# Second layer's feed-forward: both halves of the input in one 512-column matmul, with VectorE adding the parts and squaring

## The chip, the core and the metric

The kernel runs on one core of a Trainium2 chip. The metric is the device time of one execution in microseconds (us). A run's time is the median of several executions. One further execution is recorded by the hardware profiler; all rows below come from that one.

## The reference, cut to what matters

The reference is a transformer block followed by a two-layer block. Only the last part of the last layer is touched by the change:

```
def sq_relu_mlp(h, w1, w2):
    return jnp.square(jax.nn.relu(h @ w1)) @ w2
...
        h2 = adaln_norm(x, norm2_g[l], mx[3], mx[4])
        x = x + mx[5] * sq_relu_mlp(h2, w_ff1[l], w_ff2[l])
```

Here `h2` is 256 tokens by 1024 features, `w_ff1` is 1024 by 4096, and `w_ff2` is 4096 by 1024, all float32. In layer 0 the same weights also act on 256 context tokens, so its products have 512 columns; in layer 1 (the last) there are 256.

## The kernel before, in words

**Three products for one.** Every dense product is made from halves. A float32 value is split into a high half (a rounded copy in the type fp32r) and a low half (value minus high). A weight `w` and an input `x` give `wh*xh + wh*xl + wl*xh`: three matmuls of one 128x128 weight tile into one PSUM bank (lines 581, 584 and 586 in `three`). Activations are stored with features on the 128 partitions and tokens along the free dimension, so a layer-1 product has 256 columns. `HH` and `HL` hold the high and low half of the normalised input, `HIDH1` and `HIDL1` (tile HID in the trace) those of the hidden vector.

**The weight stream.** All weights come from memory as one stream of blocks of 128x1024, that is eight 128x128 tiles, 512 KB each. SyncE issues one DMA per block into four buffers `wr`. ScalarE copies a block to `wh` (three buffers, line 433), then VectorE or GpSimd subtracts to give `wl` (three buffers, line 449). `by_pool` says which of the two; in layer 1 it is GpSimd for every block behind the first group of three tiles. Every engine runs its own list in the order in which it was written. `AHEAD = 2`: on ScalarE the high half of the block that is two blocks ahead is made at a fixed place of the list. Since there are three buffers, block n waits until TensorE has finished block n - 3.

**FF1 of layer 1.** The hidden vector has 32 tiles of 128 features, f = 0 to 31. Tiles 0 to 2 are computed together in `dense_group` (lines 486, 490 and 493). From f = 3 on, `dense` computes one tile at a time: eight products over the eight input tiles. Each such f uses exactly one weight block. So there are 29 tiles, 232 products, 29 blocks. For each f the engines do this:

- ScalarE (`act_ff`): makes the high half of block f + 2; waits for the products of f; Relu from PSUM to a scratch tile `tm` (line 2780); waits for the square; copies `tm` to the high half of the hidden tile (line 2783).
- VectorE (`dve_ff`): waits for the Relu; multiplies `tm` by the PSUM bank, which gives the squared positive part (line 2798); waits for the copy; subtracts to give the low half of the hidden tile (line 2801).
- GpSimd: makes the low half of the blocks, one after the other (line 449).

On ScalarE the order is therefore: copy of f - 1, high half of block f + 2, Relu of f, copy of f. Block numbers below are the f that uses the block. The scratch ring `tm` has three tiles, the PSUM ring `main` four banks.

**FF2 of layer 1.** Eight output tiles d of 32 products each. For d = 0 to 6 `wide` is true: `three` gets an output of 512 columns, and since that is wider than `xh` it issues one matmul of `wh` with `xh` and `xl` side by side (line 578, through `beside`, which makes one access pattern of two stretches), then one of 256 columns for `wl` (line 580). The first half of the bank then holds `wh*xh + wl*xh`, the second half `wh*xl`, and VectorE adds both to the result (lines 2721 and 2727). The last tile d = 7 uses three matmuls.

Of the kernel before, what the change touches and what calls it, by code (L numbers as in the profile page):

```python
# [8 lines left out]
ALU = mybir.AluOpType  # L9
ACT = mybir.ActivationFunctionType  # L10
F32 = mybir.dt.float32
F32R = mybir.dt.float32r
# [266 lines left out]
class Program:  # L279
    def __init__(self, nc, ctx, csizes, old):  # L280
        self.nc, self.old = nc, old

        def sb(name, shape, dt=F32):
            return ctx.enter_context(nc.sbuf_tensor(name, shape, dt))
# [27 lines left out]
        self.WL = [sb(f"wl{i}", [128, 1024], F32R) for i in range(NSPL)]  # L312
        self.X = sb("X", [128, 8, 512])
        halves_at = (nc.sbuf_base + 31) // 32 * 32
        self.HH = sb("HH", [128, 8, 512], F32R)
        self.HL = sb("HL", [128, 8, 512], F32R)
        tm = [sb(f"tm{i}", [128, 512]) for i in range(3)]
        rm = [sb("rm0", [128, 512])]
        self.CT = sb("CT", [128, nconst])
# [11 lines left out]
        def at_(name, kb, shape, dt=F32):  # L331
            n = 4
            for d in shape:
# [15 lines left out]
        hl, hh = (nc.alloc_sbuf_tensor_at(n, [128, 8, 512], F32, offset=halves_at + i * 16 * KB_)  # L349
                  for n, i in (("HL2", 1), ("HH2", 0)))  # L350
# [57 lines left out]
    def low(self, n):  # L408

        if self.old is None:  # L410
            return self.c("lo_dve").at(n)
        return self.c("lo_pool" if self.by_pool(n) else "lo_dve").at(n)
# [2326 lines left out]
    def hid(self, l):  # L2739
        return (self.HIDH1, self.HIDL1) if l else (self.HIDH, self.HIDL)  # L2740

    def pe_ff(self, e, w, l, T, rhs):
        nf = 32 if l else 16
        hh, hl = self.hid(l)

        def tile(f):
            key = ("ff1", l, f)
            self.main.take(key)
            for x in self.main.before(key):
                w.wait_ge(*x)  # L2750
            return self.main.item(key)[:, 0:T], key, ("w_ff1_2", l), [(128 * f, 128 * f + 128)]

        for part in range(1 if l else 2):
            if part == 0:
                if l:
                    self.dense_group(e, w, ("ff1", l), [tile(f) for f in range(3)], rhs)
                    self.W.step(("pool on", l))
                else:
                    self.group_by_condition(e, w, ("ff1", l), [tile(f) for f in range(3)], rhs,
                                            lambda: self.pe_root_of(e, w, ("out", 0, 0), 1))  # L2760
            for f in range(nf * part, nf * part + nf):
                if f >= 3:
                    out, key, name, cols = tile(f)
                    self.dense(e, w, out, key, name, range(8), cols, rhs)
                self.tm.take(("ff1", l, f))
            self.pe_add_out(e, w, ("ff2", l, part), ("w_ff2_2", l), range(nf * part, nf * part + nf), T,
                            lambda i: (hh[:, i, :], hl[:, i, :], [self.c("g_hi").at((l, nf * part + i))],
                                       [self.c("g_lo").at((l, nf * part + i))]), (l, part) == (0, 1))

    def act_ff(self, e, w, l, T):  # L2770
        nf = 32 if l else 16
        for part in range(1 if l else 2):
            for f in range(nf * part, nf * part + nf):
                key = ("ff1", l, f)
                self.make_high(e, w, (key, 0))
                v = self.tm.item(key)[:, 0:T]
                for x in self.tm.before(key):
                    w.wait_ge(*x)
                w.wait_ge(*self.c("dense").at(key))
                e.activation(v, self.main.item(key)[:, 0:T], ACT.Relu).then_inc(*self.c("relu").mark((l, f)))  # L2780
                w.wait_ge(*self.c("dense").at(("ff2", l, 0, 7) if part else ("out", l, 0, 7) + (() if l else (1,))))
                w.wait_ge(*self.c("sqr").at((l, f)))
                ins = e.activation(self.hid(l)[0][:, f - nf * part, :], v, ACT.Copy)
                ins.then_inc(*self.c("g_hi").mark((l, f)))
                if (l, f) == (0, 2):
                    self.act_cond_silu(e, w, 2)
            self.act_add_out(e, w, ("ff2", l, part), range(nf * part, nf * part + nf), T, (l, part) == (0, 1))

    def dve_ff(self, e, w, l, T):
        nf = 32 if l else 16  # L2790
        hh, hl = self.hid(l)
        mod = iter(()) if l else self.dve_mod(e, w, 1, 2, range(48))
        for part in range(1 if l else 2):
            for f in range(nf * part, nf * part + nf):
                key = ("ff1", l, f)
                v = self.tm.item(key)[:, 0:T]
                w.wait_ge(*self.c("relu").at((l, f)))
                e.tensor_tensor(v, v, self.main.item(key)[:, 0:T], ALU.mult).then_inc(*self.c("sqr").mark((l, f)))  # L2798
                self.main.release(key, self.c("sqr"), (l, f))
                w.wait_ge(*self.c("g_hi").at((l, f)))  # L2800
                ins = e.tensor_tensor(hl[:, f - nf * part, :], v, hh[:, f - nf * part, :].bitcast(F32), ALU.subtract)
                ins.then_inc(*self.c("g_lo").mark((l, f)))
                self.tm.release(key, self.c("g_lo"), (l, f))
                for _ in range(MOD_STEPS[f]):
                    next(mod, None)
            self.dve_add_out(e, w, ("ff2", l, part), l, T, 40, (l, part) == (0, 1), mod)


# [467 lines left out]
```

## Time and profile before

| | |
|---|---|
| median of 3 executions | 1996.06 us (1993.83 to 1997.84) |
| profiled execution, its own time | 1991.99 us |
| its span in the trace | 1990.0 us |
| TensorE matmul busy | 1926.9 us (97%) |
| TensorE weight load busy | 1711.6 us (86%) |
| VectorE busy | 1235.4 us (62%) |
| ScalarE busy | 943.6 us (47%) |
| GpSimd busy | 473.7 us (24%) |

The profiled execution took 1.99 us more than its span, which is what lies around the program, and 4.07 us less than the median of the runs shown. In the rows below, PE is TensorE's matmuls, PEld its weight loads, DVE VectorE, ACT ScalarE and POOL GpSimd. FF1 of layer 1 runs from about 1808 to 1897.5 us of the span, FF2 from there to the end.

### The profile page before, as it was taken

What the parts mean: (1) busy time and instruction counts of PE and PEld (TensorE: products, weight loads), DVE (VectorE), ACT (ScalarE), POOL (GpSimd) and SP (SyncE); (2) the same over time, 40 slices, a digit from 0 to 9 for tenths busy, and PEclk for the clock granted to TensorE, in tenths of its full rate; (3) what the DMA queues carried; (4) which work ended last, traced back from release to release, by engine and by line L of the source; (5) the groups of instructions that cost most, each with busy time, mean ns of one, the idle gap of its engine ahead of it and who ended that gap; (6) DMA issues with size and microseconds to landing.
All of it is one profiled execution on the core that took longest, in us unless ns stands there. A gap on an engine that the chain in (4) does not pass through costs nothing.

```text
span 1990.0 us, 30419 instructions
## 1 busy us (share of the span) xinstructions
PE 1926.9 (97%) x12222; PEld 1711.6 (86%) x12222; DVE 1235.4 (62%) x1975; ACT 943.6 (47%) x1502; POOL 473.7 (24%) x322
## 2 busy tenths in 40 slices
PE   8998999899999999999999999999999899899999
PEld 7998888899987888787788888888888898699988
DVE  6877898679856863555663653364376947686410
ACT  5453446555456433426743531233275454765643
POOL 1211022000000000002344254555500000304887
PEclk9999999999999999999999999999999999999999
DMA  8888563467733112211133344466432233154554
GB/s 300 250 276 289 176 220 112 174 212 240 271 129 103 57 43 85 96 53 43 51 109 111 122 160 147 152 220 211 158 108 95 96 128 111 60 170 151 186 193 149
DMA packets 84636, 299.23 MB, mean 150 GB/s; under 512 B 9992, under 2 KB 13200, under 8 KB 84112
## 3 DMA queue, kind: packets, MB, share of 16 engines
q1 hardware_dynamic: 65600, 232.81, 34.2%
q0 software_dynamic: 17280, 60.95, 9.5%
q10 hardware_dynamic: 1616, 3.52, 0.5%
q8 instruction: 97, 1.59, 0.3%
q14 instruction: 43, 0.35, 0.1%
HBM read 296.18 MB, written 4.11 MB: 151 GB/s over the span
## 4 chain that ended last, share of the span: by engine, by line
PE 79%; DVE 10%; ACT 5%; issue 2%; DMA 2%; POOL 1%; DVEq 0%; SPq 0%; ACTq 0%; POOLq 0%
PE ps L586 20%; PE ps L581 20%; PE ps L584 20%; DVE wl L449 3%; PE ps L578 3%; ACT wh L433 2%; PE ps L2036 1%; PE ps L580 1%; PE ps L1236 1%; DMA dilskew<-lines 1%; PE ps L1340 1%; PE ps L1241 1%; PE ps L1238 1%; PE ps L1380 1%; PE ps L1359 1%
## 5 line engine op out<-in xcount | busy, mean ns | idle before, releaser
L581 PE MATMUL ps<-HH,wh 128*128 128x256 f32 (+1 forms) x2160 | 706.4, 327 | 7.8 <-ACT wh L433 3.8
L586 PE MATMUL ps<-HH,wl 128*128 128x256 f32 (+1 forms) x2160 | 693.0, 321 | 11.9 <-DVE wl L449 9.1
L584 PE MATMUL ps<-HL,wh 128*128 128x256 f32 (+1 forms) x2160 | 690.3, 320 | 0.0
L433 ACT ACTIVATE wh<-wr 128x1024 fp32r<-128x1024 f32 x440 | 459.1, 1053 | 345.7 <-PE ps L586 251.0
L449 DVE TENSOR_TENSOR wl<-wr,wh 128x1024 fp32r<-128x1024 f32 x301 | 367.0, 1223 | 191.8 <-ACT wh L433 191.1
L586 PEld LDWEIGHTS ps<-HH,wl 128*128 128x128 f32 x2160 | 412.9, 191 | 45.0 <-DVE wl L449 12.0
L581 PEld LDWEIGHTS ps<-HH,wh 128*128 128x128 f32 x2160 | 413.1, 191 | 43.2 <-issue 9.8
L584 PEld LDWEIGHTS ps<-HL,wh 128*128 128x128 f32 x2160 | 413.2, 191 | 30.8 <-issue 2.4
L449 POOL TENSOR_TENSOR wl<-wr,wh 128x1024 fp32r<-128x1024 f32 x139 | 338.1, 2435 | 220.3 <-ACT wh L433 218.9
L1495 POOL TENSOR_TENSOR s<-s,ST 128x512 f32<-128x512 f32 x56 | 57.4, 1041 | 688.9 <-DVE ST L1463 688.6
L1108 DVE CUSTOM_DVE_ANT_0 PROD<-WM,COND 128x1024 f32<-128x1024 f32 x104 | 127.6, 1240 | 1.3
L2727 DVE SCALAR_TENSOR_TENSOR X<-ps,MOD,X 128x256 f32<-128x256 f32 x60 | 27.0, 481 | 142.0 <-PE ps L586 141.1
L1081 POOL DMA_DIRECT2D WM<-wmod x68 | 37.7, 554 | 307.9 <-DVE MOD L1108 307.9
L586 PE MATMUL ps<-NHH,wl 128*128 128x256 f32 x352 | 99.6, 283 | 5.8 <-DVE wl L449 5.8
L581 PE MATMUL ps<-HIDH,wh 128*128 128x512 f32 (+1 forms) x272 | 103.7, 381 | 0.0
L586 PE MATMUL ps<-HIDH,wl 128*128 128x512 f32 (+1 forms) x272 | 103.0, 379 | 0.0
L584 PE MATMUL ps<-HIDL,wh 128*128 128x512 f32 (+1 forms) x272 | 102.1, 375 | 0.0
L581 PE MATMUL ps<-NHH,wh 128*128 128x256 f32 x352 | 98.7, 281 | 0.0
L584 PE MATMUL ps<-NHL,wh 128*128 128x256 f32 x352 | 98.7, 280 | 0.0
L2798 DVE TENSOR_TENSOR tm<-tm,ps 128x512 f32<-128x512 f32 (+1 forms) x64 | 35.4, 554 | 77.2 <-ACT tm L2780 77.2
L578 PE MATMUL ps<-HID,wh 128*128 128x512 f32 x224 | 78.2, 393 | 0.0
L1108 DVE CUSTOM_DVE_ANT_1 HH<-X,HL 128x1024 f32<-128x1024 f32 x56 | 68.1, 1219 | 10.5 <-DMA X<-wmod 10.5
(308 smaller groups left out, 3010.7 us busy)
## 6 DMA issues: line engine op xcount, KB each, us to landing
wr<-wstream SPq DMA_DIRECT2D x440, 512.0 KB, 3.3
WM<-wmod POOLq DMA_DIRECT2D x68, 512.0 KB, 4.2
X<-wmod POOLq DMA_DIRECT2D x28, 512.0 KB, 5.3
NAB<-naskew POOLq DMA_DIRECT2D x16, 128.0 KB, 6.0
dilskew<-lines POOLq DMA_DIRECT2D x1, 2048.0 KB, 22.7
DILB<-dilskew POOLq DMA_DIRECT2D x2, 1024.0 KB, 9.3
COND<-cond ACTq DMA_DIRECT2D x2, 1024.0 KB, 4.6
CT<-consts POOLq DMA_DIRECT2D x1, 1216.0 KB, 7.1
```

Source lines behind the costliest of these rows:

```text
L433: ins = e.activation(self.WH[i % NSPL][:, :], self.WR[n % NRAW][:, :], ACT.Copy)
L449: ins = e.tensor_tensor(self.WL[i % NSPL][:, :], self.WR[n % NRAW][:, :], self.WH[i % NSPL][:, :].bitcast(F32), ALU.subtract)
L578: e.matmul(out, wh, beside(xh, xl), start=i == 0, stop=False)
L580: return e.matmul(out[:, 0:256], wl, xh, start=False, stop=i == n_k - 1)
L581: e.matmul(out, wh, xh, start=i == 0, stop=False)
L584: e.matmul(out, wh, xl, start=False, stop=False)
L586: return e.matmul(out, wl, xh, start=False, stop=i == n_k - 1)
L1081: e.dma_start(self.mod_buffer(z, i), src).then_inc(self.mod_sem[i], 16)
L1108: ins = e.tensor_tensor_reduce(out=P, in0=self.mod_buffer(z, i), in1=S, scale=1.0, scalar=0.0, op0=ALU.mult, op1=ALU.add, accum_out=self.M ...
L1495: ins = e.tensor_tensor(sv, sv, bc(st[:, 4:4 + rows], 2, 512 // rows), ALU.mult)
L2727: ins = e.scalar_tensor_tensor(out=self.X[:, d, sl], in0=self.main.item(k)[:, sl], scalar=self.MOD[:, l, mod_i + d, c:c + 1], in1=self.X[: ...
L2798: e.tensor_tensor(v, v, self.main.item(key)[:, 0:T], ALU.mult).then_inc(*self.c("sqr").mark((l, f)))
```

## The change

For tiles f = 3 to 31 of FF1 in layer 1, the PSUM tile gets a width of 512, so that `three` takes its branch with one 512-column matmul (weight's high half, both input halves) and one 256-column matmul (weight's low half). `HH` and `HL` become two parts of one tensor, so that one access pattern reaches both. Relu on ScalarE is dropped for all 32 tiles of layer 1. VectorE copies the first half of the bank to `tm`, adds the second half (for f >= 3), and squares the positive part in place with one scalar_tensor_tensor that computes max(v, 0) * v. The low half of the hidden tile f - 1 is made after the square of tile f, and no longer directly behind the copy of f - 1.

```
-        self.HH = sb("HH", [128, 8, 512], F32R)
-        self.HL = sb("HL", [128, 8, 512], F32R)
+        halves = sb("halves", [128, 2, 8, 512], F32R)
+        self.HH, self.HL = halves[:, 0], halves[:, 1]
...
+    def two_parts(l, f):
+        return l == 1 and f >= 3
...
-            return self.main.item(key)[:, 0:T], key, ("w_ff1_2", l), [(128 * f, 128 * f + 128)]
+            width = 512 if self.two_parts(l, f) else T
+            return self.main.item(key)[:, 0:width], key, ("w_ff1_2", l), [(128 * f, 128 * f + 128)]
...
-                for x in self.tm.before(key):
-                    w.wait_ge(*x)
-                w.wait_ge(*self.c("dense").at(key))
-                e.activation(v, self.main.item(key)[:, 0:T], ACT.Relu).then_inc(*self.c("relu").mark((l, f)))
+                if l == 0:
+                    for x in self.tm.before(key):
+                        w.wait_ge(*x)
+                    w.wait_ge(*self.c("dense").at(key))
+                    e.activation(v, self.main.item(key)[:, 0:T], ACT.Relu).then_inc(*self.c("relu").mark((l, f)))
...
+    def dve_square_of_sum(self, e, w, l, f):
+        key = ("ff1", l, f)
+        v, bank = self.tm.item(key)[:, 0:256], self.main.item(key)
+        for x in self.tm.before(key):
+            w.wait_ge(*x)
+        w.wait_ge(*self.c("dense").at(key))
+        ins = e.tensor_copy(v, bank[:, 0:256])
+        if self.two_parts(l, f):
+            ins.then_inc(*self.c("x_low").mark(key))
+            w.wait_ge(*self.c("x_low").at(key))
+            ins = e.tensor_tensor(v, v, bank[:, 256:512], ALU.add)
+        ins.then_inc(*self.c("relu").mark((l, f)))
+        self.main.release(key, self.c("relu"), (l, f))
+        w.wait_ge(*self.c("relu").at((l, f)))
+        ins = e.scalar_tensor_tensor(out=v, in0=v, scalar=0.0, in1=v, op0=ALU.max, op1=ALU.mult)
+        ins.then_inc(*self.c("sqr").mark((l, f)))
...
+        def low(f, part=0):
+            key = ("ff1", l, f)
+            w.wait_ge(*self.c("g_hi").at((l, f)))
+            ins = e.tensor_tensor(hl[:, f - nf * part, :], self.tm.item(key)[:, 0:T],
+                                  hh[:, f - nf * part, :].bitcast(F32), ALU.subtract)
+            ins.then_inc(*self.c("g_lo").mark((l, f)))
+            self.tm.release(key, self.c("g_lo"), (l, f))
...
+                if l:
+                    self.dve_square_of_sum(e, w, l, f)
...
+                if l == 0:
+                    low(f, part)
+                elif f:
+                    low(f - 1)
...
+            if l:
+                low(nf - 1)
```

## Rows read from the trace of the kernel before

**Rows 1.** By stretch: length, PE, PEld, DVE, ACT, POOL busy, clock, DMA share, GB/s

```profile
1700.00:1735.00 35.00, 30.81 (x267) 23.77 (x266) 27.06 (x79) 29.18 (x81) 15.56 (x16) 1.00 0.15 51
...
1820.00:1897.50 77.50, 77.50 (x646) 77.50 (x647) 36.01 (x55) 47.01 (x80) 65.46 (x28) 1.00 0.53 184
```

**Rows 2.** Waits from 1820 to 1897.5: who waited for whom, us, times, longest

```profile
POOL wl L449 <- ACT wh L433: 12.0, 26, 0.5
```

**Rows 3.** Groups by form, 1820 to 1897.5: count, busy us, mean ns, idle before

```profile
L449 POOL TENSOR_TENSOR wl<-wr,wh 128x1024 fp32r<-128x1024 f32 x28 | 67.8, 2425 | 12.0 <-ACT wh L433 12.0
...
L433 ACT ACTIVATE wh<-wr 128x1024 fp32r<-128x1024 f32 x27 | 28.2, 1044 | 0.0
L2801 DVE TENSOR_TENSOR HID<-tm,HID 128x256 fp32r<-128x256 f32 x28 | 26.1, 933 | 13.6 <-ACT HID L2783 13.6
```

**Rows 4.** Groups by form, 1897.5 to 1976 (FF2, tiles 0 to 6)

```profile
L578 PE MATMUL ps<-HID,wh 128*128 128x512 f32 x224 | 78.2, 393 | 0.0
...
L580 PE MATMUL ps<-HID,wl 128*128 128x256 f32 x224 | 62.8, 280 | 0.0
```

**Rows 5.** Timeline of TensorE in FF1: start us, duration us, what

```profile
1831.23 0.28 PE L586 MATMUL ps<-HH,wl 128*128 128x256 f32 x1
1831.35 0.28 PE L581 MATMUL ps<-HH,wh 128*128 128x256 f32 x1
```

**Rows 6.** Timeline of ScalarE in FF1, one tile f

```profile
1831.61 0.39 ACT L2780 ACTIVATE tm<-ps 128x256 f32<-128x256 f32 x1 [0.64 <-PE ps L586]
1832.48 0.42 ACT L2783 ACTIVATE HID<-tm 128x256 fp32r<-128x256 f32 x1 [0.49 <-DVE tm L2798]
1832.81 1.04 ACT L433 ACTIVATE wh<-wr 128x1024 fp32r<-128x1024 f32 x1
```

**Rows 7.** Timeline of VectorE in FF1, the same tile

```profile
1832.03 0.42 DVE L2798 TENSOR_TENSOR tm<-tm,ps 128x256 f32<-128x256 f32 x1 [1.10 <-ACT tm L2780]
1832.93 0.87 DVE L2801 TENSOR_TENSOR HID<-tm,HID 128x256 fp32r<-128x256 f32 x1 [0.48 <-ACT HID L2783]
```

**Rows 8.** Timeline of GpSimd in FF1, two blocks' low halves

```profile
1831.12 2.41 POOL L449 TENSOR_TENSOR wl<-wr,wh 128x1024 fp32r<-128x1024 f32 x1 [0.47 <-ACT wh L433]
1833.99 2.40 POOL L449 TENSOR_TENSOR wl<-wr,wh 128x1024 fp32r<-128x1024 f32 x1 [0.47 <-ACT wh L433]
```

**Rows 9.** Timeline at the start of FF1: GpSimd's first blocks, TensorE behind them

```profile
1817.55 4.92 POOL L449 TENSOR_TENSOR wl<-wr,wh 128x1024 fp32r<-128x1024 f32 x2 [81.79 <-ACT wh L433]
...
1819.97 0.39 PE L586 MATMUL ps<-HH,wl 128*128 128x256 f32 x1 [1.66 <-POOL wl L449]
...
1819.87 5.15 POOL L449 TENSOR_TENSOR wl<-wr,wh 128x1024 fp32r<-128x1024 f32 x2
```

**Rows 10.** Groups by form of VectorE, 1600 to 1735: copy, scalar_tensor_tensor of 256 columns

```profile
L2295 DVE SCALAR_TENSOR_TENSOR tm<-tm,rm 128x256 f32<-128x256 f32 x4 | 1.7, 425 | 0.1
...
L2345 DVE COPY FR<-ps 128x256 f32<-128x256 f32 x4 | 1.7, 420 | 0.3 <-PE ps L586 0.3
```

**Rows 11.** Timeline in FF2: last matmul of a tile, VectorE behind it

```profile
1930.97 0.28 PE L580 MATMUL ps<-HID,wl 128*128 128x256 f32 x1
...
1931.29 0.48 DVE L2721 SCALAR_TENSOR_TENSOR X<-ps,MOD,X 128x256 f32<-128x256 f32 x1 [10.16 <-PE ps L580]
1931.81 0.48 DVE L2727 SCALAR_TENSOR_TENSOR X<-ps,MOD,X 128x256 f32<-128x256 f32 x1
```

**Rows 12.** Timeline in layer 0: VectorE's instruction with two SBUF inputs, GpSimd's beside it

```profile
1129.22 3.41 DVE L1108 CUSTOM_DVE_ANT_0 PROD<-WM,COND 128x1024 f32<-128x1024 f32 x1
1134.55 1.22 DVE L1108 CUSTOM_DVE_ANT_0 PROD<-WM,COND 128x1024 f32<-128x1024 f32 x1
...
1129.16 2.39 POOL L449 TENSOR_TENSOR wl<-wr,wh 128x1024 fp32r<-128x1024 f32 x1 [0.41 <-ACT wh L433]
```

**Rows 13.** Timeline of VectorE, first tiles of layer 1's FF1: back to back

```profile
1814.00 0.42 DVE L2801 TENSOR_TENSOR HID<-tm,HID 128x256 fp32r<-128x256 f32 x1 [0.48 <-ACT HID L2783]
1814.35 0.41 DVE L2798 TENSOR_TENSOR tm<-tm,ps 128x256 f32<-128x256 f32 x1
```

More of the change, by code:

```diff
@@ L2740, in hid @@
         return (self.HIDH1, self.HIDL1) if l else (self.HIDH, self.HIDL)
+    @staticmethod
+    def two_parts(l, f):
+        return l == 1 and f >= 3
     def pe_ff(self, e, w, l, T, rhs):
@@ L2795, in dve_ff @@
                 key = ("ff1", l, f)
[L2796 to L2803, printed above, removed]
+                if l:
+                    self.dve_square_of_sum(e, w, l, f)
+                else:
+                    v = self.tm.item(key)[:, 0:T]
+                    w.wait_ge(*self.c("relu").at((l, f)))
+                    e.tensor_tensor(v, v, self.main.item(key)[:, 0:T], ALU.mult).then_inc(*self.c("sqr").mark((l, f)))
+                    self.main.release(key, self.c("sqr"), (l, f))
+                if l == 0:
+                    low(f, part)
+                elif f:
+                    low(f - 1)
                 for _ in range(MOD_STEPS[f]):
                     next(mod, None)
+            if l:
+                low(nf - 1)
             self.dve_add_out(e, w, ("ff2", l, part), l, T, 40, (l, part) == (0, 1), mod)
```

## The prediction

> **What bounds the kernel now.** I read the busy times by stretch first. In FF1 of layer 1 TensorE is busy for 77.50 of 77.50 us, at a granted clock of 1.00, its level of 2.4 GHz [rows 1]. So FF1 is bound by TensorE, and only there, since GpSimd is busy for 65.46 us and ScalarE and VectorE for less. The reader should then ask which engine is nearest behind. The groups by form give it: GpSimd needs 2.425 us for the low half of one weight block [rows 3], and TensorE uses up one block per tile f. The timeline gives the period of a tile, 2.87 to 2.88 us (start to start of GpSimd's two blocks) [rows 8]. That is 0.360 us per product, 0.120 us per matmul.
>
> GpSimd's idle time is all spent on one thing: it waits for ScalarE's high half of the next block, 26 times, 12.0 us [rows 2]. So there is a chain beside TensorE: products of f done, Relu, square, copy, high half of block f + 3, low half of block f + 3. The time line of one tile shows its steps. Let M be the start of the last matmul of f = 8, 1831.23 [rows 5]. Relu starts at M + 0.38 and takes 0.39; the square starts at M + 0.80 (0.42); the copy at M + 1.25; ScalarE's next work 0.33 later, at M + 1.58, takes 1.04; GpSimd starts 0.14 after that, at M + 2.76, and ends at M + 5.16 [rows 6 to 8]. TensorE starts f = 9 at M + 0.12 [rows 5], so f = 11 at M + 5.88 and its third matmul, the first that needs the low half, at M + 6.12. The chain has 0.96 us to spare. This slack is what the change spends.
>
> One more thing is in these rows. VectorE's subtraction of 256 columns takes 0.87 us in the steady part and 933 ns in the mean [rows 7, 3], but 0.42 at the start, when GpSimd has nothing to do [rows 13]. It starts at 1832.93, GpSimd works until 1831.12 + 2.41 = 1833.53, and it ends at 1833.80, 0.27 behind that [rows 7, 8]. The instruction before it, which has one input in PSUM, runs beside the same GpSimd instruction in its plain 0.42 [rows 7]. In layer 0 an instruction with both inputs in SBUF takes 3.41 us instead of 1.22 where it starts 0.06 behind GpSimd's; it ends 1.08 behind the end of that one, so again it starts some 0.15 before GpSimd's recorded end [rows 12]. So a VectorE instruction with both inputs in SBUF is held until GpSimd's subtraction is over. Today that hits only the low half of the hidden tile, which nobody waits for.
>
> **TensorE.** The change takes one matmul and one weight load out of each of 232 products. No row shows the new pair in FF1; FF2 has it: 224 pairs fill 78.2 us, 0.349 us each [rows 4]. Against 0.360 that is 0.011 x 232 = 2.6 us less, and a tile takes 2.79 us. The other end is that FF1 keeps its 0.120 us per 256 columns, so that the wide matmul costs 0.240: nothing saved. I take FF2's pair, the same code with other tiles.
>
> The page "TensorE: Matmul & The Clock Gate" of the Trainium skill, section on the back-to-back issue gap, says that a matmul at full clock takes its columns at 2.4 GHz plus 2.5 ns. By that one instruction less saves 2.5 ns per product, an estimate of 0.6 us in all. Rows 4 and 8 put the difference at 11 ns.
>
> **The chain.** Removed from it is ScalarE's Relu (0.39). Added on VectorE is a copy out of PSUM, 420 ns for 256 columns, and the sum, 0.42 like the instruction with one PSUM input; the square becomes a scalar_tensor_tensor, 425 ns when nothing holds it [rows 10, 7]. VectorE starts 0.32 behind the start of a tile's last matmul (1930.97 to 1931.29), and a dependent instruction follows 0.04 after the end of the one before (1931.29 + 0.48 to 1931.81) [rows 11]. So the square would start at M + 0.32 + 0.42 + 0.04 + 0.42 + 0.04 = M + 1.24 and end at M + 1.67, if nothing holds it. Then 0.03 to the copy, 0.33, 1.04, 0.14 [rows 6 to 8]: GpSimd would start at M + 3.21 and end at M + 5.62. TensorE, now at 2.79 per tile, needs it at M + 0.12 + 5.58 + 0.23 = M + 5.93. Even so 0.3 us would remain.
>
> But the square now reads `v` and `v`, both in SBUF; before, one operand was the PSUM bank. At M + 1.24 GpSimd is in the middle of the block before (by the same sum, from M + 0.42 to M + 2.83). The square is held, and behind it on GpSimd's path stand the copy, the high half and GpSimd's own next block. This is the added wait; queued behind it on VectorE are the low half of f - 1 and the copy of f + 1. The trace has no such scalar_tensor_tensor beside GpSimd, so the ends are no wait at all and a wait for the rest of GpSimd's 2.41 us. I take the wait, because two other kinds of instruction with two SBUF inputs, a subtraction and a custom one, show it [rows 7, 12].
>
> The page "SBUF — State Buffer" of the Trainium skill, "Who interferes with whom", states it for VectorE instructions with two SBUF inputs in general against a GpSimd instruction that reads SBUF: the later one is blocked fully. That speaks against this change. Its other side, that GpSimd too would be blocked fully by a VectorE instruction that is first, the rows show only in part (below).
>
> **The new period.** Let E be the end of a GpSimd block during which a square was held. The square ends at E + 0.27; then 0.03 + 0.33 + 1.04 + 0.14: GpSimd starts at E + 1.81 instead of going on. In this gap VectorE does the low half (starting 0.07 before the square's end, as back-to-back instructions do [rows 13], to E + 0.62), and the next tile's copy (from E + 0.55), sum (from E + 1.01) and square, from E + 1.47. That is 0.34 before GpSimd starts, so this second square is not held, its high half comes in time, and GpSimd goes from one block straight into the next, in which the third square is held again. So two tiles cost one gap and two blocks: 1.81 + 2 x 2.41 = 6.63. GpSimd's blocks also get longer where a VectorE instruction slips in ahead: 5.15 for two against 2 x 2.41 [rows 9], 0.16 each; I add 0.2 per pair, 6.83, that is 3.42 per tile and 0.54 over today's 2.88. TensorE, with 2.79 of work, waits.
>
> From GpSimd's first block (5) to the second of FF2 (33) there are 28 such steps: 28 x 0.54 = 15.1 us. The first block itself stays where it is: VectorE is free at about 1813.1 (0.9 before the first low half [rows 13], the time of square and copy), and three copies and squares (0.88 each), one low half (0.35) and the overlaps bring its third square to about 1816.0; 1.54 later, at 1817.5, GpSimd can start, as today [rows 9]. Today TensorE already waits 1.66 us for that block [rows 9]. What follows in FF2 has no squares and is bound by TensorE, so the loss is not made up. The allocation is the same memory, and the last low half is used only by the 32nd product of FF2: nothing. The clock: TensorE would be busy for 5.58 of 6.83 us; with 30.81 of 35 us busy it keeps 1.00 [rows 1], so I add nothing.
>
> Sum: 15 us more. The profiled execution took 1991.99, which gives 2007.0; the median of the runs shown is 4.07 above it, 1996.06, which gives 2011.
>
> **The rivals.**
> - The square is not held, since both operands are the same tile and it may be read once. Nothing in the rows excludes it. Then TensorE stays the bound, the low halves on VectorE are held but not in the chain, and the 2.6 us are gained: 1993.5, nothing if FF1 keeps its pace. This is the side of "not slower".
> - Every square is held: if the second one comes over 0.34 us later than I reckon, it too falls into a GpSimd block. A tile then costs 2.41 + 1.81 = 4.22: 28 x 1.34 = 38 us more, 2034. Against it speaks only the small margin of 0.34.
> - Squares are held, but the waits fall so that fewer than one in two costs its gap: if three tiles share one gap, (1.81 + 7.23 + 0.3) / 3 = 3.11 per tile, 0.23 x 28 = 6 us more, 2002.
>
> **How the numbers follow.** Forecast 0.66, every square 0.08, fewer 0.08, not held 0.18. Some 0.2% (4 us) is what a measurement of this kernel can tell from no change. Not held gives 2.6 us at most, so 0.15 of it is "same" and 0.03 faster; slower is 0.82. The forecast's own range goes from 28 x 0.44 = 12 (no lengthened blocks) to 20 us more with 2 us of scatter, 2006 to 2018. To leave out no more than 2 in 10, the range goes down to 1992 over the cases "fewer" and "not held"; "every square" stays outside.
>
> **What would show it.** Right: the new scalar_tensor_tensor on `tm` with a mean far over 425 ns, alternating between about 0.43 and 1.6; GpSimd in pairs of blocks with a gap of about 1.8 us; TensorE waiting for GpSimd's `wl` for about 1.2 us every second tile; FF1 some 93 us long instead of 77.5; FF2 unchanged. The pair in FF1 at 0.349 us where nothing waits. Wrong: the square at 425 ns beside GpSimd's block, and TensorE busy all through FF1.

## The result and the profile after

The changed kernel takes 2008.33 us (median of five executions, 2004.79 to 2009.29) where the kernel before takes 1996.06: a ratio of 1.0053, with a 95% interval from 1.0042 to 1.0064. A second set of runs on another occasion gave 1.0063 (1.0048 to 1.0078). So the change costs 11 to 13 us. The forecast was 2011, slower.

First part 1 of the page of the changed kernel, and its stretches of FF1 and of an early stage of layer 1 (length; PE, PEld, DVE, ACT, POOL busy; granted clock; DMA share; GB/s):

```profile
PE 1929.2 (96%) x11990; PEld 1699.5 (85%) x11990; DVE 1285.1 (64%) x2036; ACT 930.1 (46%) x1470; POOL 477.4 (24%) x322
```

```profile
1470.00:1500.00 30.00, 26.89 (x153) 23.83 (x152) 16.81 (x23) 22.71 (x33) 0.00 (x0) 0.89 0.35 116
...
1820.00:1912.00 92.00, 81.26 (x447) 68.01 (x446) 82.48 (x113) 38.59 (x58) 71.90 (x29) 1.00 0.47 160
```

TensorE is no longer busy all through FF1 [rows 1]; it is idle for 10.7 of 92 us, and VectorE is now the busiest engine, at 82.48. The wait list and the groups by form of that stretch say what it is busy with:

```profile
POOL wl L449 <- ACT wh L433: 101.8, 12, 81.7
ACT HID L2791 <- DVE tm L2813: 53.6, 29, 3.7
...
PE ps L580 <- POOL wl L449: 10.7, 11, 1.9
```

```profile
L449 POOL TENSOR_TENSOR wl<-wr,wh 128x1024 fp32r<-128x1024 f32 x29 | 73.9, 2570 | 101.8 <-ACT wh L433 101.8
...
L2824 DVE TENSOR_TENSOR HID<-tm,HID 128x256 fp32r<-128x256 f32 x29 | 38.4, 1325 | 0.0
...
L2813 DVE SCALAR_TENSOR_TENSOR tm<-tm 128x256 f32<-128x256 f32 x28 | 25.8, 922 | 1.0
```

The new square takes 922 ns in the mean instead of the 425 of the same form where nothing holds it [rows 10], the hidden low half 1325 instead of 933 [rows 3]. (81.7 us of GpSimd's wait is its idle time ahead of the stage, as before [rows 9].) The trace counts the time in which an instruction is held as busy: these 57 instructions would need 24 us at 0.42 each and are recorded with 64, so some 40 of VectorE's 82.48 us are no work. ScalarE waits 53.6 us for squares, GpSimd for ScalarE, TensorE for GpSimd.

The timelines of GpSimd, VectorE and ScalarE show the pattern (start us, duration us, what):

```profile
1829.19 4.94 POOL L449 TENSOR_TENSOR wl<-wr,wh 128x1024 fp32r<-128x1024 f32 x2 [1.83 <-ACT wh L433]
1835.96 7.70 POOL L449 TENSOR_TENSOR wl<-wr,wh 128x1024 fp32r<-128x1024 f32 x3 [1.82 <-ACT wh L433]
1845.49 5.05 POOL L449 TENSOR_TENSOR wl<-wr,wh 128x1024 fp32r<-128x1024 f32 x2 [1.83 <-ACT wh L433]
```

```profile
1832.70 1.72 DVE L2813 SCALAR_TENSOR_TENSOR tm<-tm 128x256 f32<-128x256 f32 x1
1834.34 0.41 DVE L2824 TENSOR_TENSOR HID<-tm,HID 128x256 fp32r<-128x256 f32 x1
1834.67 0.41 DVE L2805 COPY tm<-ps 128x256 f32<-128x256 f32 x1
1835.12 0.42 DVE L2809 TENSOR_TENSOR tm<-tm,ps 128x256 f32<-128x256 f32 x1
1835.57 0.42 DVE L2813 SCALAR_TENSOR_TENSOR tm<-tm 128x256 f32<-128x256 f32 x1
...
1838.36 0.50 DVE L2813 SCALAR_TENSOR_TENSOR tm<-tm 128x256 f32<-128x256 f32 x1
1838.78 2.62 DVE L2824 TENSOR_TENSOR HID<-tm,HID 128x256 fp32r<-128x256 f32 x1
...
1842.51 1.44 DVE L2813 SCALAR_TENSOR_TENSOR tm<-tm 128x256 f32<-128x256 f32 x1
```

```profile
1834.45 0.42 ACT L2791 ACTIVATE HID<-tm 128x256 fp32r<-128x256 f32 x1 [3.70 <-DVE tm L2813]
1834.77 1.04 ACT L433 ACTIVATE wh<-wr 128x1024 fp32r<-128x1024 f32 x1
```

The square of 1832.70 ends at 1834.42, 0.29 behind the end of GpSimd's run of two (1834.13). GpSimd starts again at 1835.96, 1.83 behind that end: ScalarE's copy (1834.45) and high half (1834.77 to 1835.81) stand between. The next square, at 1835.57, is free. The one after that comes at 1838.36, just where GpSimd goes from the first block of its run of three to the second, and slips through the border. The low half behind it, at 1838.78, finds the second block begun and is held for 2.62 us.

**Where the time went.** FF1, from the first matmul of f = 3 to the first of FF2, runs from 1814.36 to 1909.81 in the changed kernel, 95.4 us, against 1812.15 to 1897.59 before, 85.4 us: 10 us. FF2 took 92.1 us up to the end of the last update of X, against 90.1. These 12 us agree with the 11 to 13 of the medians. The rest of the 14.2 us between the two spans, 2.2 us, lies ahead of FF1, where both kernels have the same code. In one stretch there, 1470 to 1500, the changed kernel's execution had a mean clock of 0.89 where the other had 1.00, the level of 2.4 GHz. All the profiles below have 0.89 or 0.94 in this stretch, and FF1 begins in them anywhere from 1811.83 to 1818.91 us. The kernel before has one profile only, so whether the change has any part in this is open; the medians leave little room for it.

### The profile page after: what moved, and what is told of

It is laid out like the page before. It is cut to its first block, busy times and chain, and to the rows that moved or that the text cites. A ratio compares the mean times of both kernels' runs of the same rounds, so it can differ in the third digit from the quotient of the medians.

```text
span 2004.2 us, 30014 instructions
## 1 busy us (share of the span) xinstructions
PE 1929.2 (96%) x11990; PEld 1699.5 (85%) x11990; DVE 1285.1 (64%) x2036; ACT 930.1 (46%) x1470; POOL 477.4 (24%) x322
## 4 chain that ended last, share of the span: by engine, by line
PE 77%; DVE 11%; ACT 5%; issue 3%; DMA 2%; POOL 1%; DVEq 0%; SPq 0%; ACTq 0%; POOLq 0%
PE ps L586 19%; PE ps L581 19%; PE ps L584 19%; PE ps L578 3%; DVE wl L449 3%; ACT wh L433 2%; PE ps L580 2%; DMA X<-wmod 2%; PE ps L2036 1%; PE ps L1236 1%; PE ps L1340 1%; PE ps L1241 1%; PE ps L1238 1%; POOL wl L449 1%; PE ps L1380 1%
## 5 line engine op out<-in xcount | busy, mean ns | idle before, releaser
L581 PE MATMUL ps<-halves,wh 128*128 128x256 f32 (+1 forms) x1928 | 641.1, 333 | 7.8 <-ACT wh L433 3.8
L586 PE MATMUL ps<-halves,wl 128*128 128x256 f32 (+1 forms) x1928 | 627.6, 326 | 10.1 <-DVE wl L449 9.1
L584 PE MATMUL ps<-halves,wh 128*128 128x256 f32 (+1 forms) x1928 | 624.9, 324 | 0.0
L581 PEld LDWEIGHTS ps<-halves,wh 128*128 128x128 f32 x1928 | 368.5, 191 | 43.5 <-issue 9.8
L586 PEld LDWEIGHTS ps<-halves,wl 128*128 128x128 f32 x1928 | 368.2, 191 | 43.1 <-DVE wl L449 12.0
L449 POOL TENSOR_TENSOR wl<-wr,wh 128x1024 fp32r<-128x1024 f32 x139 | 342.2, 2469 | 228.1 <-ACT wh L433 226.8
L584 PEld LDWEIGHTS ps<-halves,wh 128*128 128x128 f32 x1928 | 368.6, 191 | 31.0 <-issue 2.4
L578 PE MATMUL ps<-halves,wh 128*128 128x512 f32 x232 | 82.3, 398 | 0.0
L580 PE MATMUL ps<-halves,wl 128*128 128x256 f32 x232 | 66.3, 286 | 10.7 <-POOL wl L449 10.7
```

What stands on the lines that cost most here:

```text
L449: ins = e.tensor_tensor(self.WL[i % NSPL][:, :], self.WR[n % NRAW][:, :], self.WH[i % NSPL][:, :].bitcast(F32), ALU.subtract)
L578: e.matmul(out, wh, beside(xh, xl), start=i == 0, stop=False)
L580: return e.matmul(out[:, 0:256], wl, xh, start=False, stop=i == n_k - 1)
L581: e.matmul(out, wh, xh, start=i == 0, stop=False)
L584: e.matmul(out, wh, xl, start=False, stop=False)
L586: return e.matmul(out, wl, xh, start=False, stop=i == n_k - 1)
```

## The experiments

Each ratio is to the kernel before, measured beside it on the same chip: 1994.87 us there for the square with one SBUF input, square only, the weights' low halves on VectorE and high half first, and 1996.12 for the others. "FF1" and "FF2" are read from each trace as above, FF2 up to the end of the last update of X.

| | total us | ratio (95% interval) | FF1 us | FF2 us |
|---|---|---|---|---|
| before | 1996.06 | 1 | 85.4 | 90.1 |
| changed, again | 2008.97 | 1.0063 (1.0048 to 1.0078) | 95.3 | 92.1 |
| square with one SBUF input | 1994.26 | 0.9999 (0.9990 to 1.0009) | 84.1 | 91.1 |
| square only | 2002.24 | 1.0042 (1.0025 to 1.0059) | 91.5 | 90.9 |
| weights' low halves on VectorE | 1995.13 | 1.0000 (0.9991 to 1.0009) | 83.0 | 92.2 |
| high half first | 2005.59 | 1.0057 (1.0042 to 1.0072) | 92.1 | 93.5 |
| hidden low half from the bank | 2008.58 | 1.0068 (1.0049 to 1.0087) | 95.1 | 93.0 |
| both of the last two | 1994.64 | 0.9992 (0.9983 to 1.0002) | 82.5 | 91.1 |
| Relu back on ScalarE | 2000.47 | 1.0021 (1.0011 to 1.0030) | 85.0 | 93.3 |

**The changed kernel once more.** 

> The changed kernel as it is, as the measure for the three others of this set on the same chip. Every theory: 0.5% over the kernel before, 2004 to 2009, with GpSimd in runs of two and three blocks and gaps of 1.83 us.

It came out as expected, and its FF1 has the same length as in the first profile to 0.2 us.

**One input of the square from PSUM.**

```
-        self.main.release(key, self.c("relu"), (l, f))
         w.wait_ge(*self.c("relu").at((l, f)))
-        ins = e.scalar_tensor_tensor(out=v, in0=v, scalar=0.0, in1=v, op0=ALU.max, op1=ALU.mult)
+        ins = e.scalar_tensor_tensor(out=v, in0=v, scalar=0.0, in1=bank[:, 0:256], op0=ALU.max, op1=ALU.mult)
         ins.then_inc(*self.c("sqr").mark((l, f)))
+        self.main.release(key, self.c("sqr"), (l, f))
```

> The changed kernel, but the square takes its second factor from the first half of the PSUM bank instead of from tm (so the weight-high times input-low part is left out of one of the two factors). Same number of instructions on every engine; only the square has one input in SBUF instead of two. Theory (the square with two SBUF inputs is held by GpSimd): it takes 0.42 us always, ends at M + 1.67, TensorE does not wait for wl after the first block, a tile costs 2.83 us, total 1995 (1993 to 1997) where the kernel before has 1996. Rival (two more instructions per tile on VectorE make the chain too long, whatever they read): no difference from the changed kernel, 2004 to 2009.

The whole loss is gone. The groups by form and the waits of this kernel, 1820 to 1895:

```profile
PE ps L580 <- POOL wl L449: 1.9, 1, 1.9
```

```profile
L2824 DVE TENSOR_TENSOR HID<-tm,HID 128x256 fp32r<-128x256 f32 x27 | 35.9, 1330 | 0.0
...
L2812 DVE SCALAR_TENSOR_TENSOR tm<-tm,ps 128x256 f32<-128x256 f32 x28 | 11.8, 420 | 1.0
```

The square takes 420 ns. TensorE waits once, for GpSimd's first block, as before [rows 9]. The hidden low half is held as much as in the changed kernel (1330 ns), and costs nothing by itself. So the number of VectorE's instructions and the length of their chain are not the cause; the square's two SBUF inputs are.

**Without the wide matmul.**

```
     def two_parts(l, f):
-        return l == 1 and f >= 3
+        return False
```

> The changed kernel without its wide matmul: three matmuls of 256 columns as before, no sum on VectorE; only the Relu on ScalarE is replaced by VectorE's copy and its square from tm twice. Theory (held square): it wants to start at M + 0.78, inside GpSimd's block, so it is held and FF1 is as slow as in the changed kernel, 2004 to 2010. Rival (the wide matmul or the sum is to blame): 1995 to 1998.

Slower at 1.0042: the new square alone makes most of the loss (6 of the 10 us in FF1), with three matmuls as before and no sum. It came out 2 us below the range that I had named. The square takes 969 ns in the mean, and TensorE waits for GpSimd eight times, 1.6 us for the first block and about 0.5 us each of the other seven (waits of this kernel, 1820 to 1895):

```profile
ACT HID L2791 <- DVE tm L2813: 41.9, 16, 3.7
...
PE ps L586 <- POOL wl L449: 5.2, 8, 1.6
```

**The weights' low halves on VectorE.** On top of the edit of "high half first" below:

```
-        return at[0] < n <= at[1] and not third <= n <= W.ahead(third) or n > at[2]
+        return at[0] < n <= at[1] and not third <= n <= W.ahead(third) or n > W.upto[(("ff1", 1, 31), 0)]
...
                 elif f:
                     low(f - 1)
+                    if 2 < f < nf - 1:
+                        self.make_low(e, w, "lo_dve", (("ff1", l, f + 1), 0))
```

> The edit of high_first, and VectorE instead of GpSimd makes the low halves of the weight blocks in FF1 of layer 1. No GpSimd instruction runs there, so nothing can be held: VectorE has 0.35 + 0.46 + 0.46 + 0.35 + 1.15 = 2.8 us per tile against TensorE's 2.83. Theory: hidden low half and square at 0.42 us each, total 1995 to 1999. Rival (VectorE's load, not the hold, is the cost): 2008 or more, since this load is higher than in any other version.

With no GpSimd instruction in FF1 the square still reads `tm` twice, and nothing is held (groups by form, 1820 to 1895):

```profile
L449 DVE TENSOR_TENSOR wl<-wr,wh 128x1024 fp32r<-128x1024 f32 x27 | 32.8, 1218 | 0.0
...
L2815 DVE SCALAR_TENSOR_TENSOR tm<-tm 128x256 f32<-128x256 f32 x27 | 11.5, 425 | 0.9
...
L2826 DVE TENSOR_TENSOR HID<-tm,HID 128x256 fp32r<-128x256 f32 x27 | 11.3, 417 | 0.0
```

VectorE is busy for 72.9 of these 75 us, and the time is that of the kernel before. So it takes both partners to make the loss, and a high busy share of VectorE is not the cause. That GpSimd's instruction does the same work on VectorE in 1218 ns, against 2425 [rows 3], makes this possible.

**High half first.** ScalarE makes the high half of block f + 3 ahead of its wait for the square of f:

```
+                if l and 2 < f < nf - 1:
+                    self.make_high(e, w, (("ff1", l, f + 1), 0))
                 w.wait_ge(*self.c("sqr").at((l, f)))
```

> The changed kernel, but ScalarE makes the high half of block f + 3 before it waits for the square of f, not behind the copy of f. The square still reads tm twice. Theory (the loss comes through the chain square, copy, high half, GpSimd): GpSimd starts at M + 1.57, before which the square (from M + 1.24) has already begun, so neither waits for the other; TensorE is the bound; total 1995 (1993 to 1997), with squares at 0.43 us. Rival (squares and GpSimd's blocks exclude each other and together fill more than a tile, wherever they stand): 2000 or more, squares still held.

Here my theory failed, and the time is in the rival's range. FF1 is 3 us shorter than in the changed kernel, but FF2 is 1.4 us longer, with one wait of TensorE for GpSimd of 2.0 us near its start, and the total is still at 1.0057. GpSimd's, ScalarE's and VectorE's timelines of this kernel:

```profile
1845.85 7.74 POOL L449 TENSOR_TENSOR wl<-wr,wh 128x1024 fp32r<-128x1024 f32 x3 [1.83 <-ACT wh L433]
```

```profile
1844.34 0.42 ACT L2793 ACTIVATE HID<-tm 128x256 fp32r<-128x256 f32 x1 [3.73 <-DVE tm L2815]
1844.66 1.05 ACT L433 ACTIVATE wh<-wr 128x1024 fp32r<-128x1024 f32 x1
```

```profile
1847.05 1.70 DVE L2815 SCALAR_TENSOR_TENSOR tm<-tm 128x256 f32<-128x256 f32 x1
1848.68 2.63 DVE L2826 TENSOR_TENSOR HID<-tm,HID 128x256 fp32r<-128x256 f32 x1
...
1852.14 1.73 DVE L2815 SCALAR_TENSOR_TENSOR tm<-tm 128x256 f32<-128x256 f32 x1
1853.79 0.41 DVE L2826 TENSOR_TENSOR HID<-tm,HID 128x256 fp32r<-128x256 f32 x1
```

The square gets through at a border between two blocks, but the low half behind it finds the next block begun and is held for all of it. A tile has two instructions with two SBUF inputs, and a border lets one pass. So VectorE falls behind: its copy out of PSUM starts 0.4 us behind the start of the tile's last matmul for f = 4 and 5, but 1.8 to 4.2 us behind it from f = 9 on, where a tile of TensorE is 2.8 us. ScalarE's copy of f then holds up even the high half that I had moved forward by one: it waits 3.73 us for the square, and the high half at 1844.66 for the copy. The rival had the squares and GpSimd's blocks together fill more than a tile; the second of the next two kernels goes against this, since it has the same squares and takes no longer than the kernel before. From this came a second theory: there are two costs, the chain through ScalarE's order, and two held instructions for one place. The next two kernels separate them.

**The hidden low half from the bank.**

```
-        self.main.release(key, self.c("relu"), (l, f))
...
-            ins = e.tensor_tensor(hl[:, f - nf * part, :], self.tm.item(key)[:, 0:T],
+            src = self.main if l else self.tm
+            ins = e.tensor_tensor(hl[:, f - nf * part, :], src.item(key)[:, 0:T],
...
+            if l:
+                self.main.release(key, self.c("g_lo"), (l, f))
```

This edit alone is the first kernel; the second has the edit of "high half first" as well. In both, what is computed as the low half lacks the Relu, the square and the second half of the bank.

> The changed kernel, but the low half of the hidden tile is computed from the PSUM bank instead of from tm (what it yields is not the reference's low half). So VectorE has one instruction per tile with two SBUF inputs, the square, instead of two. ScalarE's order is the changed kernel's. Theory 1 (two separate costs: the chain through ScalarE's order, and that at the border of two back-to-back GpSimd blocks only one held instruction gets through while a tile has two): the chain is still there, so a held square still opens a gap of 1.8 us; 2002 to 2008, the low half at 0.42 us. Rival 2 (the chain alone): the same, 2002 to 2008. Rival 3 (only the number of held instructions per tile counts): 1993 to 1997.

> low_from_bank and high_first together: one instruction with two SBUF inputs per tile, and ScalarE makes the high half of block f + 3 before it waits for the square of f. Theory 1 (two costs): both are gone, TensorE is the bound, 1993 to 1997, squares held now and then without any wait of TensorE. Rival 2 (chain alone, which high_first did not really break): like high_first, 2003 to 2008. Rival 3 (number of held instructions alone): 1993 to 1997, and low_from_bank too.

The first kernel is as slow as the changed one (1.0068; 2008.58, just over my range). The second has nothing left of the loss (0.9992). One held instruction is not enough to be fast, and neither is the order of ScalarE; both together are. So rivals 2 and 3 fall. The first kernel (GpSimd, then VectorE, then the square's group) shows the cycle that I had forecast for the changed kernel, in its plain form:

```profile
1839.61 4.77 POOL L449 TENSOR_TENSOR wl<-wr,wh 128x1024 fp32r<-128x1024 f32 x2 [1.82 <-ACT wh L433]
1846.21 4.75 POOL L449 TENSOR_TENSOR wl<-wr,wh 128x1024 fp32r<-128x1024 f32 x2 [1.82 <-ACT wh L433]
```

```profile
1842.19 2.47 DVE L2812 SCALAR_TENSOR_TENSOR tm<-tm 128x256 f32<-128x256 f32 x1
...
1845.93 0.42 DVE L2812 SCALAR_TENSOR_TENSOR tm<-tm 128x256 f32<-128x256 f32 x1
...
1848.71 2.54 DVE L2812 SCALAR_TENSOR_TENSOR tm<-tm 128x256 f32<-128x256 f32 x1
```

Always two blocks and a gap of 1.82, 6.60 us for two tiles (1839.61 to 1846.21), where the prediction had 6.63 before its allowance for longer blocks; every second square is held. FF1 is no shorter than in the changed kernel (95.1 against 95.3), though no hidden low half is held any more: with ScalarE's order as it is there, taking that hold away gains nothing. In the second kernel GpSimd makes its first eight blocks without a pause, and the one square of a tile gets in at the borders. From 1839.97 on most blocks stand alone, and the square has room before each (GpSimd, then the square):

```profile
1839.97 2.41 POOL L449 TENSOR_TENSOR wl<-wr,wh 128x1024 fp32r<-128x1024 f32 x1 [0.35 <-ACT wh L433]
1842.74 2.42 POOL L449 TENSOR_TENSOR wl<-wr,wh 128x1024 fp32r<-128x1024 f32 x1 [0.36 <-ACT wh L433]
```

```profile
L2814 DVE SCALAR_TENSOR_TENSOR tm<-tm 128x256 f32<-128x256 f32 x26 | 13.7, 529 | 0.9
```

**Relu back on ScalarE.** A version that computes all and keeps the wide matmul; ScalarE also makes the high half of block f + 3 ahead of its Relu:

```
+                    w.wait_ge(*self.c("x_low").at((key, "sum")))
...
+            e.tensor_copy(v, bank[:, 256:512]).then_inc(*self.c("x_low").mark(key))
             w.wait_ge(*self.c("x_low").at(key))
...
+            ins = e.tensor_tensor(bank[:, 0:256], v, bank[:, 0:256], ALU.add)
+            ins.then_inc(*self.c("x_low").mark((key, "sum")))
         w.wait_ge(*self.c("relu").at((l, f)))
...
+        ins = e.tensor_tensor(v, v, bank[:, 0:256], ALU.mult)
```

> A repaired version that computes everything: the wide matmul stays; VectorE copies the second half of the bank and writes the sum back into the first half in PSUM; ScalarE makes Relu from PSUM to tm as before the change; VectorE multiplies tm by the bank. ScalarE makes the high half of block f + 3 before its Relu. One held instruction per tile is left, the hidden low half. Theory 1: TensorE is the bound at 2.83 us per tile, 1 to 2 us under the kernel before, which can't be told from it: 1992 to 1997. Rival (five dependent steps per tile over two engines are too long a chain in any order): 2000 or more.

At 1.0021 it is clearly better than the changed kernel but not as good as before. The time is above the range of my theory and just inside the rival's. Its GpSimd goes in pairs with a gap of 0.95 (4.95 + 0.95, or 2.95 us per tile), a little more than TensorE's need:

```profile
1837.91 4.95 POOL L449 TENSOR_TENSOR wl<-wr,wh 128x1024 fp32r<-128x1024 f32 x2 [0.94 <-ACT wh L433]
1843.81 4.95 POOL L449 TENSOR_TENSOR wl<-wr,wh 128x1024 fp32r<-128x1024 f32 x2 [0.95 <-ACT wh L433]
```

Behind the first block TensorE still does not wait for it within FF1, which takes 85.0 us. What this execution loses lies in FF2, 93.3 us against 90.1: GpSimd idles 3.49 us there for a high half that ScalarE makes only behind its copy of the last hidden tile, and TensorE waits 2.0 us. The hidden low half is held in this kernel too (1334 ns in the mean), so the runs do not tell the length of the chain from the hold. Its executions scatter from 1996.52 to 2004.27, and the profiled one, with a span of 1994.6, is the fastest. Where the slower ones lose their time is open. No version here beats the kernel before by more than its measurement can tell.

## Why the prediction was right, step by step

- **TensorE is the bound, with 0.96 us to spare in the chain.** Right. With an unheld square and everything else of the change in place, TensorE waits no more than before.
- **The wide matmul saves 2.6 us, or nothing.** In FF1 it does save, in the whole kernel nothing that can be told. With TensorE's wait for the first block taken off, a product of FF1 takes 0.361 us in the kernel before (85.4 less 1.7 us over 232 products), 0.354 us with the square's one SBUF input and with the weights' low halves on VectorE, and 0.350 us in the kernel with both of the last two edits: 1.5 to 2.7 us saved, where the prediction had 2.6. But in these three kernels FF2, which is not changed, takes 1.0 to 2.1 us more (below), and their totals are 0.9992 to 1.0000. The page "TensorE: Matmul & The Clock Gate" of the Trainium skill, section on the back-to-back issue gap, gives the 2.5 ns from which the prediction estimated 0.6 us for a matmul by itself, and says that in a stream with weight loads the formula counts too little for few columns and too much for many. The traces of FF1 show more than 0.6 us.
- **The square is held.** Right, the step on which all hung. It was inferred from a subtraction and a custom instruction; a scalar_tensor_tensor whose two inputs are the same tile is held in the same way, to 0.29 us behind GpSimd's end (0.27 forecast). Taking away one SBUF input, or GpSimd, takes away the whole loss. The rule of the page "SBUF — State Buffer" of the Trainium skill, section "Who interferes with whom", that the one that comes later is blocked fully, agrees with the traces for VectorE's side. For the other side GpSimd's block takes 2570 ns in the mean instead of 2425 [rows 3]. Two blocks in a row take 4.76 us where no held instruction passes between them (hidden low half from the bank), and 4.94 to 5.07 where one does (changed kernel): GpSimd loses 0.2 to 0.3 us by an instruction of 0.42.
- **A gap of 1.81 us.** Right: 1.82 and 1.83, in every gap.
- **One gap in two tiles, 3.42 us per tile.** The term that was mis-sized, by the number of tiles to a gap. GpSimd makes 28 blocks from 1819.66 to 1911.14 (eleven runs of three and two by turns), 3.27 us each: 0.39 over 2.88 and not 0.54, so 10.9 us instead of 15.1. I had let every second square meet a block and open a gap. But in a run of three the square of 1838.36 slips through the border between two blocks, and the gap comes every 2.5 tiles: 12 of the 29 squares are held for long. Against that the blocks are a little longer, 2.55 against my 2.51. That a square would meet such a border at just the right moment was nowhere in the sum, and where squares do not, the period is the one forecast (6.60 us for two tiles, hidden low half from the bank).
- **Nothing after FF1.** Wrong by 1.9 us, the same in both profiles of the changed kernel. 0.7 us of it is one more wait for GpSimd, and 1.0 us is a pace of 0.353 us per pair instead of 0.349 [rows 4], over 224 pairs, in a stage whose code is not changed. It is no scatter between executions: the kernel before, square only and Relu back have 0.349, the seven other profiles 0.353, all at a granted clock of 1.00. Its cause is open. So the forecast total, 15 us more where 12 were lost, came as near as it did partly by luck: 4 us too many in FF1 stood against 2 too few in FF2.
- **The rival "not held"** is excluded; **"every square held"** (2034) did not come: the square that had to be ahead of GpSimd's next start was so by 0.39 us (1835.57) and by 0.15 (1845.34) by turns, so the margin of 0.34 held, but every other time only just; **"fewer"** is in part what happened, at 2.5 tiles to a gap.
- **The signs.** The squares take 0.42 to 0.52 or 1.3 to 1.7 us, where I had 0.43 and 1.6. TensorE's waits are 1.07 and 0.69 us by turns, two in five tiles, where I had 1.2 in every second. "FF1 some 93 us long instead of 77.5" counts from 1820 on; FF1 became 10 us longer and not 15.

## What to carry to other kernels

Before VectorE gets an instruction with both inputs in SBUF in a stage where GpSimd works nearly all the time, ask what waits for it: the same instruction with one input in PSUM ran in 0.42 us, this one in 0.92. What it costs is decided by what follows on the other engines' lists; here a wait of 0.5 us in the mean held up the copy, the next weight block and GpSimd itself, and cost 10 us in 29 tiles. Count such instructions per period of the other engine: between two back-to-back GpSimd blocks one got through here.

## What the runs showed of the hardware

- A held VectorE instruction of 0.42 us ends 0.27 to 0.29 us behind GpSimd's recorded end, whether it waited 1 or 2 us. By these numbers, an estimate, it starts about 0.14 before that end.
- Where GpSimd goes from block to block without a pause, a waiting VectorE instruction gets in between (the square of 1838.36), but the next one, whose record starts 0.07 to 0.08 us before the first ends, does not: it is held for the whole block, 2.6 us.
- GpSimd's two blocks with one such instruction in between take 4.94 to 5.07 us instead of 4.76.
- The same pairs of matmuls in FF2, at a granted clock of 1.00, had a pace of 0.349 us in three kernels and 0.353 in six others that differ from them only in FF1. What sets it is open.
